# A two-layer transformer trunk on one core: stick-breaking mask moved from TensorE to VectorE, weight tiles given other places, splits put in another order

## What is computed

```python
z = q @ k.T                                   # q already scaled by 1/sqrt(128)
visible = (key position >= 0) & (key position < query position)
sp = where(visible, softplus(z), 0)
tail[t, s] = sum of sp[t, j] for j from s to t - 1
w = exp(where(visible, z - tail, -inf))
out = w @ v
```

## Time and profile before

| | |
|---|---|
| median of 3 runs | 911.52 us |
| the profiled execution: its own time | 910.97 us |
| its span, first to last instruction | 909.1 us |
| TensorE busy with matmuls | 899.3 us (99% of the span), 7211 matmuls |
| VectorE busy | 549.1 us (60%) |
| ScalarE busy | 428.1 us (47%) |
| GpSimd busy | 62.8 us (7%) |
| mean granted TensorE clock | 0.997 |
| DMA | 153 MB, mean 168 GB/s |

### The profile page before, as it was taken

One profiled execution on the slowest core, in us unless ns is written; L12 is line 12 of the kernel. 1 busy time (PEld: TensorE's weight loads), 2 busy tenths in 40 slices (PEclk: granted clock), 3 DMA queues, 4 the chain that ended last, 5 costly groups with the idle time before them and its releaser, 6 DMA issues.

```text
span 909.1 us, 17887 instructions
## 1 busy us (share of the span) xinstructions
PE 899.3 (99%) x7211; PEld 865.8 (95%) x7211; DVE 549.1 (60%) x720; ACT 428.1 (47%) x683; POOL 62.8 (7%) x85
## 2 busy tenths in 40 slices
PE   9999999999999999899999999999999999999997
PEld 9999999999999999899999999999999999998886
DVE  6578667666765766775746364554636355555546
ACT  6556455545655434375444353535344443435421
POOL 1322033213200000000000000000000000000000
PEclk9999999999999999999999999999999999999998
DMA  9775475446442545414453444445353534454622
GB/s 351 234 229 168 149 223 147 143 155 193 155 144 97 201 168 198 172 47 186 163 209 138 169 154 157 166 141 182 138 185 138 183 140 158 165 198 174 231 92 93
DMA packets 25255, 153.05 MB, mean 168 GB/s; under 512 B 3410, under 2 KB 3938, under 8 KB 8708
## 3 DMA queue, kind: packets, MB, share of 16 engines
q1 hardware_dynamic: 21600, 142.19, 43.4%
q0 software_dynamic: 2896, 7.70, 4.2%
q10 hardware_dynamic: 724, 2.66, 0.8%
HBM read 150.36 MB, written 2.18 MB: 168 GB/s over the span
## 4 chain that ended last, share of the span: by engine, by line
PE 93%; DVE 2%; DMA 2%; ACT 1%; issue 1%; SPq 0%; DVEq 0%
PE bank L328 67%; PE bank L700 10%; DMA raw<-chunks 2%; PE bank L483 2%; PE bank L443 2%; DVE w_lo L1065 1%; PE bank L645 1%; PE bank L644 1%; PE bank L647 1%; ACT w_hi L779 1%; PE bank L568 1%; PE bank L585 1%; PE bank L612 1%; PE bank L349 1%; PE bank L350 1%
## 5 line engine op out<-in xcount | busy, mean ns | idle before, releaser
L1065 DVE TENSOR_TENSOR w_lo<-raw,w_hi 128x2048 fp32r<-128x2048 f32 x126 | 290.7, 2312 | 232.1 <-ACT w_hi L779 199.4
L328 PE MATMUL bank<-x_hi,w_hi 128*128 128x272 f32 (+1 forms) x1472 | 425.6, 289 | 1.2 <-ACT work L784 0.9
L328 PE MATMUL bank<-x_hi,w_lo 128*128 128x272 f32 (+1 forms) x1472 | 421.5, 286 | 0.0
L328 PE MATMUL bank<-x_lo,w_hi 128*128 128x272 f32 (+1 forms) x1472 | 421.2, 286 | 0.0
L779 ACT ACTIVATE w_hi<-raw 128x2048 fp32r<-128x2048 f32 x114 | 217.6, 1911 | 159.0 <-PE bank L328 106.7
L328 PEld LDWEIGHTS bank<-x_hi,w_hi 128*128 128x128 f32 x1472 | 277.4, 188 | 2.6 <-issue 1.9
L328 PEld LDWEIGHTS bank<-x_hi,w_lo 128*128 128x128 f32 x1472 | 277.3, 188 | 0.0
L328 PEld LDWEIGHTS bank<-x_lo,w_hi 128*128 128x128 f32 x1472 | 277.1, 188 | 0.0
L328 PE MATMUL bank<-og_hi,w_hi 128*128 128x272 f32 x240 | 70.2, 292 | 0.3 <-DVE h L1239 0.3
L328 PE MATMUL bank<-og_hi,w_lo 128*128 128x272 f32 x240 | 69.4, 289 | 0.0
L328 PE MATMUL bank<-og_lo,w_hi 128*128 128x272 f32 x240 | 69.1, 288 | 0.0
(11 more groups left out here) (245 smaller groups left out, 1025.4 us busy)
## 6 DMA issues: line engine op xcount, KB each, us to landing
raw<-chunks SPq DMA_DIRECT2D x128, 1024.0 KB, 4.8
work<-bias_table POOLq DMA_DIRECT2D x8, 512.0 KB, 5.7
work<-chunks SPq DMA_DIRECT2D x4, 512.0 KB, 12.4
work<-bias_table POOLq DMA_DIRECT2D x8, 256.0 KB, 6.6
work<-ln_rows ACTq DMA_DIRECT2D x1, 2048.0 KB, 7.5
out<-work SPq DMA_DIRECT2D x8, 256.0 KB, 2.3
h<-xT SPq DMA_DIRECT2D x2, 544.0 KB, 9.3
raw<-chunks SPq DMA_DIRECT2D x4, 256.0 KB, 5.1
```

The source lines that it names most:

```text
L328: last = mm(o, l, r, start=(kt == 0 and n == 0), stop=(kt == KT - 1 and n == 2))
L1065: V.tensor_tensor(lo_part, raw[:, half, :, :], hi_part.bitcast(f32), ALU.subtract) \
```

## The change

- The mask of z: the three mask matmuls of an iteration go. VectorE takes the minimum of z and a matrix `cap` (-1e30 where masked, 3e38 elsewhere), in PSUM, in three instructions, placed in its program between the splits lo(P+3, 1) and lo(P+4, 0). ScalarE's L992 waits for them.
- The four slots of `w_hi` and `w_lo` are given to layer B's chunks in another order (`B_SLOTS`), and `FREE` changes with it.
- The splits around the layer change and in `body_b(0)` stand at other places of the programs of ScalarE and VectorE. In `body_b(i)`, i > 0, ScalarE's order stays, and VectorE's stays but for the three minima.
- Between the layers, the `mean_rows` matmuls come after the two `on_tokens` groups, `centre` runs one pair ahead and not two, and there are 4 idle matmuls in place of the first 9.

```diff
-SPINS, SPINS_2 = 9, 5
+SPINS, SPINS_2 = 4, 5
...
+        B_SLOTS = (2, 0, 3, 1)
...
+            if layer_b or isinstance(P, int) and P >= P_B + 2:
+                at = B_SLOTS[at]
...
             project(P_B - 1, og_hi, og_lo, ALL)
             pe.wait_ge(c_summed, KT - 1)
-            mm(mean_rows, mean_w[:], ln["c_sum"], start=True, stop=False)
             on_tokens(token_mean, ln["c_sum"], first=True)
             pe.wait_ge(tile_free[1], P_B)
-            on_tokens(token_mean, h[:, KT - 1, :], last=True)
-            mm(mean_rows, mean_w[:], h[:, KT - 1, :], start=False, stop=True).then_inc(mean_ready, 1)
+            on_tokens(token_mean, h[:, KT - 1, :], last=True).then_inc(mean_ready, 1)
             pe.wait_ge(sq_summed, KT - 1)
             on_tokens(token_sq, ln["sq_sum"], first=True)
             pe.wait_ge(sq_ready, KT)
             on_tokens(token_sq, ln["sq"][:, 1, :], last=True).then_inc(mean_ready, 1)
+            for n, rows in enumerate((ln["c_sum"], h[:, KT - 1, :])):
+                m = mm(mean_rows, mean_w[:], rows, start=(n == 0), stop=(n == 1))
+            m.then_inc(mean_ready, 1)
...
                     mm(z[:, 0:B_K1], k[:, 0:128], q, start=True, stop=False)
-                    mm(z[:, B_K1:B_K2], k[:, 128:256], q[:, B_Q1:SEQ], start=False, stop=False)
-                    m = mm(both(z[:, 0:128], B_K1), ident_r[:], mask_r[:, 0:256].rearrange("p (a b) -> p a b", b=128),
-                           start=False, stop=(u == 0))
+                    m = mm(z[:, B_K1:B_K2], k[:, 128:256], q[:, B_Q1:SEQ], start=False, stop=(u == 0))
...
-                mm(z, b["kT"][:, B_ENDS], b["q"][:, :, B_Q2:SEQ], start=False, stop=False)
-                mm(z, ident_r[:], mask_r[:, 256:256 + B_L], start=False, stop=True).then_inc(z_ready, 1)
+                mm(z, b["kT"][:, B_ENDS], b["q"][:, :, B_Q2:SEQ], start=False, stop=True).then_inc(z_ready, 1)
...
         FREE = {(P_B, 1): (tile_full[1], P_B - 2), (P_B + 1, 0): (half_used, P_B - 1),
-                (P_B + 1, 1): (tile_full[1], P_B - 1), (P_B + 2, 0): (half_used, P_B + 2),
-                (P_B + 2, 1): (tile_full[1], P_B + 2)}
+                (P_B + 1, 1): (tile_full[1], P_B - 1), (P_B + 2, 0): (half_used, P_B),
+                (P_B + 2, 1): (half_used, P_B + 2), (P_B + 3, 0): (tile_full[1], P_B + 2)}
...
                 split_hi(P + 2, 0)
-                if P == P_B - 2:
-                    split_hi(P_B, 1)
+                if P >= P_B - 3:
+                    split_hi(P + 2, 1)
                 for u in range(2):
                     square(2 + 2 * n, u, tile_free[u], P + 1)
-                if P < P_B - 2:
+                if P < P_B - 3:
                     split_hi(P + 2, 1)
...
-                if n == 5:
-                    split_hi(P_B + 2, 0)
-                elif n >= 2:
-                    offset(n - 2)
-            for n in (3, 6, 7):
+                if n in (2, 5):
+                    split_hi(P_B + 2, n // 3)
+                elif n > 2:
+                    offset((n - 3, n - 4)[n > 5])
+            for n in range(4, 8):
                 offset(n)
...
                 if isinstance(i, int):
-                    split_hi(P + 2, 1)
-                    split_hi(P + 3, 0)
+                    split_hi(P + 3, 0, True)
+                split_hi(P + 3, 1, True)
...
-                    act.wait_ge(z_ready, 2 * i + n + 1)
+                    act.wait_ge(z_capped, 3 * i + 2 * n + 1)
                     A(w, z, ACT.Abs).then_inc(sp_abs, 1)
...
                 if isinstance(i, int):
-                    split_hi(P + 3, 1)
-                    split_hi(P + 4, 0)
-                else:
-                    split_hi(P + 4, 1)
-                    split_hi(P + 5, 0)
+                    split_hi(P + 4, 0, True)
+                split_hi(P + 4, 1, True)
+                split_hi(P + 5, 0, True)
...
             def out_a(P, t):
-                if P == P_B - 2:
-                    split_lo(P_B, 0)
-                for u in range(2):
+                if P >= P_B - 3:
+                    split_lo(P + 2, 0)
+                for u in range(2):
+                    if u and P == P_B - 2:
+                        split_lo(P_B, 1)
                     combined(P, u, t + u)
-                    if u == 0 and P < P_B - 2:
+                    if u == 0 and P < P_B - 3:
                         split_lo(P + 2, 0)
+                    if u and P == P_B - 3:
+                        split_lo(P + 2, 1)
...
-            centre(0)
             dve.wait_ge(ln_step, 4)
             dve.wait_ge(rs_guess, 2)
             newton(ln["rstd"], ln["var"], ln["tmp"], ln_step, 4)
-            centre(1)
+            dve.wait_ge(mean_ready, 4)
+            centre(0)
             dve.wait_ge(rstd_ready, 1)
             for n in range(KT // 2):
                 scaled(n)
-                if n + 2 < KT // 2:
-                    centre(n + 2)
+                if n + 1 < KT // 2:
+                    centre(n + 1)
                 rest(n)
-                if n == KT // 2 - 2:
+                if n == KT // 2 - 3:
                     split_lo(P_B + 2, 0)
...
-                ahead = ((3, 1), (4, 0))
-                for p, half in ((2, 1), (3, 0)) if isinstance(i, int) else ((2, 0), (2, 1), (3, 0)) + ahead:
-                    split_lo(P + p, half)
+                if not isinstance(i, int):
+                    split_lo(P + 2, 0, True)
+                split_lo(P + 2, 1, True)
+                split_lo(P + 3, 0, True)
+                split_lo(P + 3, 1, True)
+                for u in range(2):
+                    dve.wait_ge(z_ready, 2 * i + u + 1)
+                    z = both(z_bank[u][:, 0:128], B_K1)
+                    V.tensor_tensor(z, z, cap[:, 0:256].rearrange("p (a b) -> p a b", b=128), ALU.min) \
+                     .then_inc(z_capped, 1)
+                z = z_bank[1][:, B_K2:B_K2 + B_L]
+                V.tensor_tensor(z, z, cap[:, 256:256 + B_L], ALU.min).then_inc(z_capped, 1)
+                if not isinstance(i, int):
+                    split_lo(P + 4, 0, True)
...
+                    if u == 0 and isinstance(i, int):
+                        split_lo(P + 4, 0, True)
+                split_lo(P + 4, 1, True)
+                split_lo(P + 5, 0, True)
```

More of the change, by code:

```diff
@@ L29 @@
 NEG = -1e30
+BIG = 3e38
 A_HD = 64
@@ L157, in trunk, with split_views @@
         mean_rows, rstd_rows = bank[2][:, 0:T], bank[4][:, 0:T]
-        def split_views(P, half):
+        B_SLOTS = (2, 0, 3, 1)
+        def split_views(P, half, layer_b=False):
             at = 2 * half_slot(P) + half
+            if layer_b or isinstance(P, int) and P >= P_B + 2:
+                at = B_SLOTS[at]
             if isinstance(P, int):
@@ L294, in project @@
             def project(P, m_hi, m_lo, cols, x_from=None, between=None, token_major=False, late=None,
-                        banks=None, free_at=None, early=None):
+                        banks=None, free_at=None, early=None, layer_b=False):
                 for half in range(2):
                     pe.wait_ge(lo_ready, 2 * P + half - 3)
-                    hi_part, lo_part = split_views(P, half)
+                    hi_part, lo_part = split_views(P, half, layer_b)
                     order = [(u, k) for u in range(2) for k in range(HALF)]
@@ L659, in body_b @@
                 else:
-                    project(P, x_hi, x_lo, SEQ_COLS)
-                    project(P + 1, x_hi, x_lo, ALL)
+                    project(P, x_hi, x_lo, SEQ_COLS, layer_b=True)
+                    project(P + 1, x_hi, x_lo, ALL, layer_b=True)
                 project(P + 2, x_hi, x_lo, ALL, between=lambda: scores_b(i),
-                        banks=v_acc_0 if isinstance(i, int) else None)
+                        banks=v_acc_0 if isinstance(i, int) else None, layer_b=True)
                 def mid():
@@ L667, in mid @@
                     turn_values(i)
-                project(P + 3, x_hi, x_lo, SEQ_COLS, between=mid)
+                project(P + 3, x_hi, x_lo, SEQ_COLS, between=mid, layer_b=True)
                 attend_b(i)
@@ L694, in row_quarter @@
                     kt = QUARTER * c + k
-                    whi, wlo = (w[:, c].rearrange("p a b -> p (a b)")[:, k * RW + cols.start:k * RW + cols.stop]
+                    whi, wlo = (w[:, B_SLOTS[c]].rearrange("p a b -> p (a b)")[:, k * RW + cols.start:k * RW + cols.stop]
                                 for w in (w_hi, w_lo))
@@ L774, in _, with split_hi @@
             nc.scalar.preload_act_table_set("exp_and_others")
-            def split_hi(P, half):
+            def split_hi(P, half, layer_b=False):
                 act.wait_ge(raw_loaded[half], 16 * (P - 1))
                 wait_slot_free(act, P, half)
-                A(split_views(P, half)[0], raw[:, half, :, :], ACT.Copy).then_inc(hi_ready, 1)
+                A(split_views(P, half, layer_b)[0], raw[:, half, :, :], ACT.Copy).then_inc(hi_ready, 1)
             def evac(P, u, dst, cols, scale=1.0):
@@ L817, in _ @@
```

(26 more changed lines are left out.)

25 lines of the change are left out of this document (9 added, 16 removed).

## The result

The changed kernel takes 905.21 us (median of 6 runs, 904.96 to 905.33) where the one before takes 911.28 (6 runs, 910.74 to 911.93): ratio 0.9932, 95% interval 0.9921 to 0.9942. The profiled execution took 904.98 us with a span of 903.1.

The account below looks back on a forecast made before the run. TensorE's work and its few waits around the layer change were taken to set the time; 2.8 + 0.55 + 1.4 + 0.5 + 1.1 = 6.4 us off the 911.5 median gave 905.1 us, range 904.2 to 907.3.

Parts of the forecast that it names:

- Mask on TensorE: Layer B's score block, without its mask matmuls, falls from 1.84 to 1.49 us in each of 8 iterations: 2.8 us.
- The minima: Three on VectorE between scores and abs each iteration, 0.43, 0.43 and 0.2 us, 1.1 in all, said to cost nothing.
- Stall at 367: TensorE's 0.28 us wait at 367.44 in layer A's output projection goes because splits come earlier: 0.55 us.
- LayerNorm: Between layers, the copy L1294 starts at 377.3, not 379.31, without two mean_rows groups in front: 1.4 us beyond the stall.
- First iterations: Layer B's iterations 0 and 1: earlier splits remove waits at the gate (0.5 us) and before P = 31 (1.1 us).
- v's bank: Iteration 0: v's u = 1 copy frees its bank about 422.2, just when P = 29 wants it; uncounted, up to 0.3.
- the tails 6.9 us later: VectorE's softplus split ends at 474.64, TensorE asks at 481.56, so the minima's delay fits each iteration and costs nothing.
- the slower rival: Minima make the tails late each iteration; decides from 6.9 us of delay, needs 7.7 to end above 911.5; chance 0.03.
- the doubled price: Twice the row, 0.86 us, bounds a minimum's slow PSUM write; the three take up to 2.1 us an iteration.
- The clock: Rival: fewer idle matmuls let the clock fall to half for 5.4 us in layer B, costing 2.7: 907.8 us; chance 0.03.

Follow-up runs that it names:

- no_l: The changed kernel with the LayerNorm's part as before (mean rows before token sums, centre two pairs ahead, 9 idle matmuls); 906.02 us, ratio 0.9941.
- part L: The LayerNorm's part: mean rows after token sums, centre one pair ahead, 4 idle matmuls for 9; alone on the kernel before 911.08 us, ratio 0.9997.
- s_only: The changed kernel with mask back on TensorE and LayerNorm as before, so only weight places and split order are new; 908.66 us, ratio 0.9967.
- v_first: The changed kernel with iteration 0's split lo(P+4, 0) after both copies of v, not between them; 905.13 us, ratio 0.9936.
- caps2: The changed kernel with each of the two large minima done twice; 906.50 us, one run.
- caps6: The changed kernel with each of the two large minima done 6 times, each waiting for the one before; 947.19 us, one run.
- m_only: The kernel before with only the mask moved to minima on VectorE; 909.53 us against 911.68, ratio 0.9977.
- no_spins: The changed kernel without any of the 9 idle matmuls left between the layers; 906.76 us, ratio 0.9945.
- small_pe: The changed kernel with only the 32-column mask back on TensorE as one matmul; 906.27 us, ratio 0.9947.
- no_m: The changed kernel with the mask back as matmuls on TensorE; 907.81 us, ratio 0.9963.

## Why the prediction was right

The time (905.21 for 905.1) and the terms came out as written, by rows of the traces. That the time is met to 0.1 us has some luck in it: the change gained 6.1 us and not 6.4, from a median before that was 911.28 and not 911.52. The terms:

- **Mask on TensorE**, 2.8: measured 8 x (52.57 - 52.22) = 2.8. Taking the block from a like block was right; counting columns would have missed the small one. The minima took the 0.43, 0.43 and 0.19 us that were forecast.
- **Stall at 367**, 0.55: the last projection matmul stands at 376.48 before and 376.33 after, less the 0.4 of a late start-up: 0.54.
- **LayerNorm**, 1.4: measured 1.44. The way as the prediction followed it is right, but where it names the cause of the 2.0 us it names two groups of mean rows at 0.66. Only the second stood in front of the copy (no_l), and part L is worth 0.7; the other half is that the last tiles' additions no longer stand behind lo(27, 1) (s_only).
- **First iterations**, 0.5 + 1.1 less up to 0.3 for v's bank: IT0 fell by 1.71, of which 0.35 are the mask, so 1.36. The wait at v's second tile that it named came, with 0.22 (v_first).
- Sum of these 6.1; the spans differ by 6.0. The start-up took 0.4 more, and from the last score block to the end it took 0.2 less, beyond that block's mask. In the last stage the clock fell later (0.71 in its window, 0.50 in that of the earlier trace rows), which may be the reason. The start-up shifts by more than this among kernels that are alike up to there; that the end owes nothing to the change is argued, not shown.

**One step was wrong though the time was right**: that what follows the minima has room because TensorE asks for the tails 6.9 us later, and with it the point from which the slower rival decides. It followed the softplus to the tails and did not ask what else is queued behind it on VectorE: the copy of v, which TensorE wants first. The slack is 0.5 us. The cost of the minima was still nothing, for the other reason that the prediction gives: the split behind them waits for ScalarE's hi anyway. In iteration 2 of the kernel before:

```profile
522.71 2.29 DVE L1065 TENSOR_TENSOR w_lo<-raw,w_hi 128x2048 fp32r<-128x2048 f32 x1 [3.48 <-ACT w_hi L779]
...
527.16 0.43 DVE L1357 COPY work<-bank 128x272 f32<-128x272 f32 x1
```

The minima took place in those 3.48 us of idle. The score block starts at 520.50 there and the copy ends 7.09 us later; after the change it is 7.08. The copy didn't move; TensorE came 0.35 us earlier, so the slack fell from 0.9 to 0.5. But with the doubled price that the prediction called harmless it is used up (caps2), and caps6's 4.6 us more an iteration cost 42 us. The minima were free by a smaller margin than the prediction believed, and that is luck.

**The clock** had 3 in 100. The change's own six runs are all within 0.4 us, and its profiled one kept 1.00; yet it fell in the profiled executions of m_only, s_only and no_spins. The first two have all 14 idle matmuls, so the fall doesn't need fewer of them, and why it comes in some executions and not in others stays open. The prediction's argument, that the stage before had kept 1.00, rested on one trace.

## What to carry to other kernels

When something is put into an in-order queue, look for the earliest deadline of everything behind it, not for that of its own result: here a 0.4 us copy that only frees a bank was due 5.6 us before the tails. Cost a removed matmul by the difference of two like blocks, since one with weights of its own has a price that its columns don't show. Idle matmuls cost nothing where no one waits for them, and without them three of four runs were 1.1 to 2.1 us slower; but they are no guarantee, and a trace in which the clock holds doesn't say that it always will.

## What the runs showed of the hardware

- A float32-reduced matmul of 32 columns with other weights than the one before added 0.11 us (small_pe), one of 256 columns 0.12 us, worked out from no_m and small_pe.
- In caps6 a matmul that waited for VectorE's copy started 0.15 us after the copy's end.
- A minimum over 128 x 256 in and out of PSUM took 0.43 us on VectorE, as long as an addition of 272 with its result in SBUF, and twelve in a row, each waiting for the one before, 5.43 us.
- The granted clock after the LayerNorm's gaps was 1.00 in most profiled executions, but 0.50 for about 3.4 us in m_only and s_only (QK 1.34 and 1.35 us longer) and for 6.8 us in no_spins (2.59 longer). The Trainium skill (TensorE: Matmul & The Clock Gate, "HAM oscillation — how this bites in real kernels") tells of the same fall after idle gaps, which in its kernel are waits for DMA of several us. These traces show it with waits of at most 1.35 us between the layers, and in m_only and s_only with waits as long as in the kernel before, where the clock held; the measurement decides. In caps6, with a wait of 3.5 us in each iteration, the mean clock of the steady part was 0.97.
